# Seven half-size products for each pair of up and gate tiles in three gated feed-forward stages

## What is computed

```python
def conv_ffn(x, w_up, conv_w, conv_b, w_down):      # stages 0 and 1
    h = x @ w_up                                    # 1024 -> 2 * 2816
    hp = jnp.pad(h, ((0, 0), (CONV_W - 1, 0), (0, 0)))
    hc = conv_b
    for j in range(CONV_W):
        hc = hc + hp[:, j:j + L] * conv_w[j]
    u, g = jnp.split(hc, 2, axis=-1)
    return (jax.nn.silu(g) * u) @ w_down
```

## Time and profile before

| | us |
|---|---|
| median of three runs (lowest, highest) | 2308.55 (2307.75, 2308.59) |
| profiled execution, its time | 2309.27 |
| its span, first to last instruction | 2307.3 |
| PE, DVE, ACT busy in it | 2287.0, 1285.3, 909.8 |
| granted clock of TensorE, share of full speed | 0.999 |

### The profile page before, as it was taken

The page is one execution under the profiler, slowest core; times in us unless marked ns, Lnnn a source line. Parts: engine busy times, 40 slices in busy tenths (PEclk is TensorE's granted clock), DMA queues, the critical chain, the costliest instruction groups (busy, mean ns, idle before and its releaser), DMA issues.

```text
span 2307.3 us, 36725 instructions
## 1 busy us (share of the span) xinstructions
PE 2287.0 (99%) x15423; PEld 2038.2 (88%) x15423; DVE 1285.3 (56%) x2258; ACT 909.8 (39%) x1566; POOL 34.5 (1%) x75
## 2 busy tenths in 40 slices
PE   9999999999999999999999999999999999999998
PEld 7798999999997898999899788978898888888887
DVE  5356576446643465766366566869455455443443
ACT  5356544224333465543144443223244444221232
POOL 2000000000000000000000000000000000000001
PEclk9999999999999999999999999999999999999999
DMA  4221223222312221323223222223222232332331
GB/s 137 92 72 47 86 83 100 87 80 92 110 58 74 93 61 43 102 92 107 77 92 109 80 75 74 91 85 98 92 65 65 65 101 92 100 110 74 100 109 55
DMA packets 57910, 197.47 MB, mean 86 GB/s; under 512 B 8545, under 2 KB 12547, under 8 KB 57747
## 3 DMA queue, kind: packets, MB, share of 16 engines
q1 hardware_dynamic: 55827, 189.73, 25.6%
q0 software_dynamic: 1344, 4.36, 0.6%
q10 hardware_dynamic: 576, 1.05, 0.1%
HBM read 192.98 MB, written 2.13 MB: 85 GB/s over the span
## 4 chain that ended last, share of the span: by engine, by line
PE 93%; DVE 3%; ACT 2%; issue 1%; DMA 0%; POOL 0%; SPq 0%; ACTq 0%; DVEq 0%; POOLq 0%
PE G L1079 76%; PE G L1153 7%; PE X L1365 1%; PE X L1320 1%; PE X L1447 1%; PE X L1343 1%; DVE wL L1950 1%; PE X L1431 1%; PE X L1148 1%; ACT wH L1489 1%; PE X L1416 1%; PE X L1079 1%; PE X L1403 0%; PE X L1279 0%; PE X L1375 0%
## 5 line engine op out<-in xcount | busy, mean ns | idle before, releaser
L1079 PE MATMUL G<-aH,wH 128*128 128x264 f32 (+2 forms) x2992 | 759.0, 316 | 4.0 <-DVE wL L1950 3.6
L1079 PE MATMUL G<-aL,wH 128*128 128x264 f32 (+2 forms) x2992 | 738.1, 309 | 0.0
L1079 PE MATMUL G<-aH,wL 128*128 128x264 f32 (+2 forms) x2992 | 737.5, 309 | 0.0
L1489 ACT ACTIVATE wH<-raw 128x512 fp32r<-128x512 f32 (+3 forms) x477 | 386.9, 829 | 666.6 <-PE G L1079 612.1
L1950 DVE TENSOR_TENSOR wL<-raw,wH 128x512 fp32r<-128x512 f32 (+3 forms) x477 | 443.7, 941 | 207.1 <-ACT wH L1489 205.1
L1079 PEld LDWEIGHTS G<-aH,wH 128*128 128x128 f32 x2992 | 488.0, 189 | 43.5 <-issue 9.9
L1079 PEld LDWEIGHTS G<-aH,wL 128*128 128x128 f32 x2992 | 485.6, 188 | 29.4
L1079 PEld LDWEIGHTS G<-aL,wH 128*128 128x128 f32 x2992 | 486.2, 188 | 26.9 <-issue 0.2
L2102 DVE TENSOR_TENSOR hT<-G,hT 128x528 f32<-128x528 f32 (+1 forms) x83 | 58.1, 700 | 215.8 <-PE G L1079 215.8
L1079 PE MATMUL G<-hidH,wH 128*128 128x264 f32 (+1 forms) x528 | 140.7, 321 | 1.4 <-DVE hidL L2186 1.4
L1079 PE MATMUL G<-hidL,wH 128*128 128x264 f32 (+1 forms) x528 | 141.1, 322 | 0.0
(11 more groups left out here) (348 smaller groups left out, 2689.9 us busy)
## 6 DMA issues: line engine op xcount, KB each, us to landing
raw<-weights SPq DMA_DIRECT2D x276, 512.0 KB, 3.5
raw<-weights SPq DMA_DIRECT2D x48, 704.0 KB, 4.0
raw<-weights SPq DMA_DIRECT2D x12, 384.0 KB, 3.1
negc<-sums POOLq DMA_DIRECT2D x16, 264.0 KB, 4.4
out_t<-hT SPq DMA_DIRECT2D x16, 128.0 KB, 1.8
raw<-weights SPq DMA_DIRECT2D x14, 128.0 KB, 2.1
hT<-x_t ACTq DMA_DIRECT2D x4, 256.0 KB, 4.8
hT<-x_t SPq DMA_DIRECT2D x4, 256.0 KB, 7.0
```

The lines of the kernel that those rows point to most:

```text
L1079: done = e.matmul(m.pair(i)[0:M, bank, 0:n], a[:, k, 0:M], b[:, kx, lo - t0:lo - t0 + n], start=(k == 0 and c == 0), stop=(k == nk - 1 and ...
L1489: e.activation(m.high(i)[:, c], m.raw[:, r, c], ACT.Copy).then_inc(s.w_hi, 1)
```

## The change

In each stage, from the fourth pair on (19 of 22 pairs), up tile U and gate tile W of a pair are multiplied together by Strassen's method: the weights are a 2 x 2 of (up, gate) by (first, second four blocks), the operand a 2 x 2 of (first, second four blocks) by (first, second half of the tokens). Seven products of 4 blocks x 3 x 1, 12 matmuls each, take the place of 96 (48 in stage 2), with 264, 258 and 256 columns. Their role is ("seven", stage, half, pair, p), p in 1 to 7.

- Weights. Products 1, 2 and 3 take plain blocks. For 5, 6 and 4 the block that product 1, 5 and 6 used is kept in raw, and Pool issues a DMA that adds the next block to it (accum_op add), as soon as the split of the one before is done. For 7 SP loads a block into its own slot and Pool adds a second. raw is used as 11 slots of 512 columns: three for the chain 1, 5, 6, 4, two for 7, three for 3, three for 2. So a pair has four plain and four adding loads, of 256 KB each, where it had two loads of 512 KB.
- Split weights. wH and wL are used as five places of 512 columns; a product's split comes up to four products ahead.
- Operands. In pairs 1 and 2 of half 0 DVE writes the normed x in full (norm7, eight instructions of 528, 516 or 512 columns) and four sums of its quarters (sum7, 1056, 1032 or 1024 columns); high7 and low7 split the seven operands. Three of these lie in aH and aL and are made after the last plain tile (last_operands), behind a flush().
- Results. Products 1, 2, 5, 6, 7, 3, 4 go to G and X in PSUM; some accumulate on an earlier one there. ACT copies 1, 5, 6 and 4 out (p1st, p5th, u2nd, c21), DVE adds 2, 7 and 3 (c11, c22, c12). Some sums have their sign turned; the convolution's weights, or silu's scale, are negated for that. Convolution, silu, gate and hidden split follow one piece a product (pieces).

The core of the diff:

```diff
+def by_seven(first):
+    out, pairs = [], list(range(first, 11))
+    if pairs:
+        out += [(pairs[0], 1), (pairs[0], 2), (pairs[0], 5)]
+    for n, jj in enumerate(pairs):
+        if n + 2 < len(pairs):
+            nx = pairs[n + 1]
+            out += [(jj, 6), (nx, 1), (jj, 7), (nx, 2), (nx, 5), (jj, 3), (jj, 4)]
+        elif n + 2 == len(pairs):
+            nx = pairs[n + 1]
+            out += [(jj, 6), (nx, 1), (jj, 7), (nx, 2), (nx, 5), (jj, 3), (nx, 6), (jj, 4), (nx, 7), (nx, 3), (nx, 4)]
+    return out
...
+        for jj, p in by_seven(plain):
+            of, k0 = {1: (u, 0), 2: (u, 4), 5: (g, 0), 6: (g, 4), 7: (g, 0), 4: (u, 4), 3: (g, 4)}[p]
+            fm(("seven", f, half, jj, p), of[0], of[1], of[2] + 128 * (11 * half + jj), nk=4, k0=k0)
...
+        if role[0] == "seven":
+            if ROLE[i - 1][0] != "seven":
+                run = 1
+                while ROLE[i + run][0] == "seven":
+                    run += 1
+                k = -run % 5
+            at, k, n = 512 * k, (k + 1) % 5, n + n % 2
+        else:
+            at, n = WMAX * (n % NW), n + 1
...
+    def seven():
+        while ROLE[state["next"]][0] == "seven":
+            i = state["next"]
+            _, f, half, jj, p = ROLE[i]
+            if ROLE[i - 1][0] != "seven":
+                flush()
+            state["next"] += 1
+            while state["split"] < len(PLAN) and WAS.get(state["split"], -1) < i and ROLE[state["split"]][0] != "out":
+                step("split", state["split"], 0, 1)
+                state["split"] += 1
+            if pieces:
+                step(*pieces.popleft())
+            step("prod7", f, half, jj, p)
+            step({1: "p1st", 2: "c11", 5: "p5th", 6: "u2nd", 7: "c22", 3: "c12", 4: "c21"}[p], f, half, jj)
+            if p == 3 and f < 2:
+                pieces.append(("conv7", f, half, jj, 1))
+            if p == 4:
+                pieces.extend([("conv7", f, half, jj, 0)] if f < 2 else [])
+                pieces.extend(("%s7" % what, f, half, jj) for what in ("silu", "gate", "hidh", "hidl"))
+            yield
...
+    def last_operands(f):
+        for p in 7, 4, 3:
+            step("high7", f, p)
+            step("low7", f, p)
...
+                if l in SEVEN:
+                    if not half:
+                        flush()
+                        last_operands(l)
+                        if l:
+                            step("meta2")
+                    yield from seven()
...
+    def prod7(f, half, jj, p):
...
+        for k in range(4):
+            for c, (a, b) in enumerate(((wh, xh), (wh, xl), (wl, xh))):
+                done = e.matmul(out, a[:, k, :], b[:, k, :], start=(p in (1, 2, 5) and k == 0 and c == 0),
+                                stop=(k == 3 and c == 2), skip_group_check=p not in (1, 2, 5))
+        done.then_inc(s.chunk, 1)
...
+    def high7(f, p):
+        e.wait_ge(s.seven_in, SUMS_IN["norm7", f, 7] if p in (1, 2, 4) else SUMS_IN["sum7", f, p])
+        if p == 7:
+            e.wait_ge(s.chunk, AT["seven", f, 0, SEVEN[f], 1])
+        e.activation(m.seven_operand(f, p)[0], m.seven_source(f, p), ACT.Copy).then_inc(s.seven_hi, 1)
...
+    def split(i, q, parts):
+        if q < parts - 1:
+            return
+        for c in ADD_AT.get(i, ()):
+            block = c
+            if c in SECOND:
+                block, first, times = SECOND[c]
+                e.wait_ge(s.ring[first], 16 * times)
+            else:
+                e.wait_ge(s.w_lo, SPLIT_DONE[RAWWAS[c]][-1])
+            e.dma_start(m.raw(c), weights(W, block), accum_op=ALU.add).then_inc(s.ring[RING[c]], 16)
...
-        if q == parts - 1:
-            load(i + NR)
+            for c in LOAD_AT.get(i, ()):
+                load(c)
```

More of the change, by code:

```diff
@@ L168, in places @@
 def places():
-    place, was, n, last = {}, {}, 0, {}
+    place, was, n = {}, {}, 0
+    last, k = [-1] * (NW * WMAX), 0
     for i, role in enumerate(ROLE):
@@ L610, in fg @@
             for half in range(2):
-                for jj in range(11):
+                made = operands(2) if 2 in SEVEN and not half else []
+                for jj in range(11 if 2 not in SEVEN else SEVEN[2] * (1 - half)):
                     first = half + jj == 0
-                    yield from fm(hold=first)
-                    yield from fm(hook=("rms", ("ffn2",)) if first else None)
+                    now, made = ([], made) if first else (made[:16], made[16:])
+                    yield from fm(hold=first, before=dict(enumerate(now[0:8])))
+                    yield from fm(hook=("rms", ("ffn2",)) if first else None, before=dict(enumerate(now[8:16])))
+                assert not made
+                if 2 in SEVEN:
+                    if not half:
+                        flush()
+                        last_operands(2)
+                    yield from seven()
                 for _ in range(8 - half):
@@ L737, in banks @@
     for i, role in enumerate(ROLE):
+        if role[0] == "seven":
+            first = AT[role[:4] + (1,)]
+            if i == first:
+                out[i], g = g, 1 - g
+            else:
+                out[i] = out[first]
+            continue
         if role[0] == "gq" and role[2] == 1:
@@ L748 @@
 FIRST = {"ffglr", "ki"}
+SUMS_DVE = count_of(("c11", "c22", "c12"))
+SUMS_ACT = count_of(("p1st", "p5th", "u2nd", "c21"))
+SUMS_IN = count_of(("norm7", "sum7"))
 def first_of_stage(role):
@@ L799, in new @@
             return ctx.enter_context(nc.semaphore(name))
-        self.ring = [new(f"ring{i}") for i in range(NR)]
+        self.ring = [new(f"ring{i}") for i in range(NR + 12)]
         self.vecs = new("vecs")
@@ new lines, in low7, with c11 @@
+    def low7(f, p):
+        high, low = m.seven_operand(f, p)
+        e.wait_ge(s.seven_hi, NTH["high7", f, p])
+        e.tensor_tensor(low, m.seven_source(f, p), high.bitcast(F32), ALU.subtract).then_inc(s.seven_lo, 1)
+    def c11(f, half, jj):
+        i, n = AT["seven", f, half, jj, 2], STAGE[f][1]
+        out = m.pair_out(f, jj, 0)[:, 0:n]
+        e.wait_ge(s.sums_act, SUMS_ACT["p1st", f, half, jj])
+        e.wait_ge(s.chunk, i + 1)
+        e.tensor_tensor(out, out, X[:, 2 + BANK[i], 0:n], ALU.add).then_inc(s.sums_dve, 1)
@@ new lines, in conv7 @@
+    def conv7(f, half, jj, which):
+        n, col, slot = nth7(f, half, jj), 11 * half + jj + NFF * which, 2 * (jj % 2) + which
+        o = NM if f else 0
+        av = m.Av[:, slot, o:L]
+        e.wait_ge(s.conv0, 2 * n + 2 - which)
+        e.scalar_tensor_tensor(out=av, in0=m.Hs[:, slot, 1 + o:1 + L], scalar=m.vc(("cw", f, 1), col), in1=av,
+                               op0=ALU.mult, op1=ALU.add).then_inc(*own.one())
+        e.wait_ge(own.sem, own.n)
+        e.scalar_tensor_tensor(out=av, in0=m.Hs[:, slot, o:L], scalar=m.vc(("cw", f, 0), col), in1=av,
+                               op0=ALU.mult, op1=ALU.add).then_inc(s.taps, 1)
```

343 lines of the change are left out of this document (285 added, 58 removed).

## The result

| | us |
|---|---|
| kernel before, median of 4 runs (lowest, highest) | 2308.57 (2307.75, 2309.11) |
| changed kernel, median of 4 runs (lowest, highest) | 2616.65 (2612.65, 2618.85) |
| ratio, 95% interval | 1.1333 (1.1313 to 1.1353) |
| changed kernel, profiled: time, span, granted clock | 2617.55, 2616.3, 0.946 |

A forecast was written before the change was run, and what follows sets the result against it. TensorE (PE) was taken to bound the kernel, and the chain through the adding loads to decide the changed one. 2309.27 + 20 for the pairs + 61 for the starts = 2390, as median 2389 us; range 2275 to 2475.

The forecast's parts named there:

- PE's gain: Steady pairs: 84 matmuls for 96, 10.28 us a pair (10.08 in stage 2); 75 us less if PE paced all.
- DVE's 9.7: DVE's work a pair in stages 0 and 1: 10.5 us by durations, about 9.7 with overlap.
- ACT's 8.8: ACT's splits, copies out of PSUM, convolution starts, silu and hid copy: 8.8 us of 10.28 a pair.
- 2D + 3.97: Least time of a pair through two chained adding loads, ACT's splits and hid copy; 11.67 us in stage 0.
- 2D + 4.41: The same loop in stage 2, with DVE's hidL and c11 in place of the copy: 12.11 us a pair.
- D: Time from the end of a split to the landed sum as ACT sees it: 3.85 us, with a landing of 3.7.
- The upper bound of 6.5: Upper bound of an adding load's landing: 6.5 us, the slowest of Pool's 264 KB loads, four at once.
- rival 3: Long sums: adding loads land in 4.4 us, +80 on the forecast, 2469 us; chance 0.15.
- The starts: Starts and exits of the six runs of products: +61 us in sum, between 35 and 75.
- (a): DVE's norm7, lows and sums in pairs 1 and 2: stalls of 5 us (2.5 in stage 2), 13 in sum.
- (b): First product of half 0: flush and last operands precede product 1's split, done at 10.5 us; 36 us in sum.
- rival 1: Quick sums, landing at most 3.0 us, PE paces the pairs: 2275 to 2301 us; chance 0.37.

The follow-up runs named there:

- the last kernel: Against the stage-2-only kernel with DVE's sums, redealt slots and later sum for product 7: results' piece put ahead of splits and sums; 2317.91 us (1.0040).

## Why the prediction was wrong in size

- **PE's gain** was right: 10.21, 10.07, 9.98 us a pair without adds. So was DVE's 9.7 (9.4 to 9.6); ACT's 8.8 was high (38.69 / 52 x 10.39 = 7.7), since its queued instructions overlap as DVE's do (two splits of 0.62 take 1.14).
- **The mechanism of the pair** was right: 2D + 3.97 in stages 0 and 1. Four runs move one term of it each and the period follows: 12.5 with 4.1 twice, 11.7 to 12.2 with half the bytes, 14.0 to 14.5 where an add outside it goes, 11.3 to 11.7 where ACT's order no longer closes it. Stage 2's 2D + 4.41 was tested less: with its landings of 5.9 and 4.1 (medians) it gives 14.7 for the 14.5 to 14.6 of the changed kernel, but without the add for 4 the pair took 0.4 to 0.9 us more than it gives.
- **D was mis-sized**, and it is the larger error: 3.7 us for both landings, where one is 4.1 and the other mostly 6.2 to 6.6. The first was near. The second failed at a sentence that named the danger and priced it wrongly: the add for 5'' goes out a microsecond behind the one for 4', and its price was read from two plain loads issued together, 3.6 to 3.8 both the earlier trace rows. Plain loads don't hold each other up so (median 3.0 us over all 228 of Pool's, the longest 4.9); adds do. The upper bound of 6.5 was in the text, and rival 3 took 4.4 of it. The pairs cost +175, where +20 was forecast.
- **What an add costs.** The DMA engines' time in Pool's queue is 6.9 us for four adds against 3.6 for four plain loads, and the landing rises by 1.05 us for 128 KB added. The Trainium skill (Collectives: The Full Stack, "The bandwidth ceiling: the fold count and why AG ≠ RS ≠ AR") lays the slowness of the adding step of a collective to two source reads: the trace agrees in size, with 1.9, and shows no reads by themselves. By its fit (DMA: Bandwidth & Descriptors, "Anatomy of one DMA — SWDGE (gpsimd) path") 512 KB took 3.2 us in the prediction; measured are 4.1. The half adds leave 2.0 us for no bytes, so its fixed part agrees and its rate for bytes does not.
- **The starts were mis-sized**: +61 forecast, 133 measured, 83 to 90 of them without any add. In (a) and (b) the backlog of DVE at the first product was taken as 5 us in stages 0 and 1; in stage 0 it is 10.7 (327.8 to 338.54), and the tail of 5 us and three operands of 1.06 stand behind it. The split of product 1 is done 21.2 us after the last plain matmul, where (b) had 10.5. DVE's timeline, from the evacuation to the splits:

```profile
338.54 0.70 DVE L2400 TENSOR_TENSOR Hs<-G,rbc 128x528 f32<-128x528 f32 x1
...
344.80 1.26 DVE L2605 TENSOR_TENSOR aL<-sums,aH 128x1056 fp32r<-128x1056 f32 x1 [0.27 <-ACT aH L1990]
...
348.31 1.29 DVE L2275 TENSOR_TENSOR wL<-raw,wH 128x512 fp32r<-128x512 f32 x2
```

The order explains 20 us of it (2616.65 to 2596.24, 2319.51 to 2300.08). Of what comes with the adds, some 30 us lie in the first two periods of each run, which take 15 to 18.5 us (starts of product 6 on PE) and had no term.

- **The clock had no term.** Behind the stall the granted clock is 0.50 (1.2 GHz), and it falls again behind shorter ones (0.50 from 580.70 to 583.90 us, behind a stall of 4.63): 0.93 and 0.87 in the mean of the two windows above, 1.00 in the earlier trace rows. The same 15651 matmuls are busy 2328.4 us for 2229.3 without adds. So of the 298 us between these two spans, 99 are slower matmuls and 199 idle time of PE. How much would be left with a full clock no run separates, since each that shortens the stalls also raises the clock, and a faster PE might only wait longer for the same loads.
- **What no rival said**: that with no adds at all the kernel is still slower than before (2319.51), where rival 1 put quick sums at 2275 to 2301. The starts eat PE's gain of 79 us; with them reordered the three stages end 8.9 us ahead (2300.08).

## What to carry to other kernels

Where a chain runs through a DMA several times a period, price each pass by what is queued just ahead of it, and by what kind that is: here one issue in another place was worth 72 us, and one split in another place 167. A method that saves multiplications moves them to adders: count the adders' work at the start of a stage as closely as in its steady part, and ask first what is won if the new work costs nothing (here 9 us of 2309, and only with the starts reordered). When one wait is removed from an engine's strict order, look for the next consumer of that engine: in the last kernel it was there at once.

## What the runs showed of the hardware

- An adding load of 256 KB from DRAM into SBUF lands in 4.1 us alone, 128 KB in 3.05, and mostly 5.6 to 6.8 us (median 6.3, at most 7.6) when issued 0.5 to 1.5 us behind another; a plain one in 3.0. Its issue holds Pool for 0.87 us, a plain one's for 0.54.
- Adds fill the DMA engines 1.9 times as much as plain loads of the same bytes from the same queue (15.6% of 2616.3 us for 9.0% of 2413.2, less 0.6%). With adds among the loads the engines are 0.87 busy at 177 GB/s, where plain traffic shows 0.59 at 189.
- Pool's tensor_tensor of 128x512 on SBUF takes 1.3 to 1.7 us beside a busy DVE and delays DVE instructions with two SBUF inputs that start under it (0.77 becomes 1.66). The Trainium skill (SBUF — State Buffer, "SBUF: two separate sides") says of the port pair that the two engines share that, of two such instructions, "the other fully blocks"; the trace agrees in size, four sums to some 3.9 us of DVE a pair (0.97 x 13.9 less 9.6).
- Behind a stall of 21.3 us the granted clock was 0.50 in the first three microseconds of matmuls, and 0.98 from 355 to 360 us; in two long stretches with stalls of some us in every pair it was 0.93 and 0.87 in the mean, and 1.00 in the kernel before, which has no such stalls there.
